# Five instead of four seven-product pairs in the up chunks of a split-precision decoder layer, the gate product moved to GpSimd

## The reference, cut to what matters

```python
D_MODEL, SEQ, D_FF = 2048, 256, 5632
def swiglu(x, wg, wu, wd):
    return (jax.nn.silu(x @ wg) * (x @ wu)) @ wd
...
f = swiglu(rmsnorm(h, ffn1_pre_g[l]), ffn1_wg[l], ffn1_wu[l], ffn1_wd[l])
h = h + FFN_RES_WEIGHT * rmsnorm(f, ffn1_post_g[l])
...  # a mixing part: sparse attention beside a convolution module, gated, times w_out
f = swiglu(rmsnorm(h, ffn2_pre_g[l]), ffn2_wg[l], ffn2_wu[l], ffn2_wd[l])
h = h + FFN_RES_WEIGHT * rmsnorm(f, ffn2_post_g[l])
```

## Time and profile before

| | us |
|---|---|
| median of 3 runs | 2064.92 (2064.72 to 2065.35) |
| the profiled execution, own time | 2066.93 |
| its span | 2065.3 |
| PE busy | 2051.3 (99%) |
| DVE busy | 1761.8 (85%) |
| ACT busy | 1163.3 (56%) |
| POOL busy | 97.2 (5%) |

### The profile page before, as it was taken

One profiled execution on the slowest core, in us unless ns is written; L12 is line 12 of the kernel. 1 busy time (PEld: TensorE's weight loads), 2 busy tenths in 40 slices (PEclk: granted clock), 3 DMA queues, 4 the chain that ended last, 5 costly groups with the idle time before them and its releaser, 6 DMA issues.

```text
span 2065.3 us, 26384 instructions
## 1 busy us (share of the span) xinstructions
PE 2051.3 (99%) x9238; PEld 1694.5 (82%) x9238; DVE 1761.8 (85%) x2039; ACT 1163.3 (56%) x1292; POOL 97.2 (5%) x134
## 2 busy tenths in 40 slices
PE   9999999999999999999999999999999999999998
PEld 7888888888888788888788888888888888888886
DVE  6999899989888858998687566878999899989897
ACT  6565665556555554444466444565656566666463
POOL 0010001000000000100000000000000000000000
PEclk9999999999999999999999999999999999999999
DMA  9777777765666666776555666567777777846664
GB/s 332 228 233 228 225 215 237 235 203 177 196 198 204 187 186 192 203 207 184 172 170 180 184 191 213 185 229 227 227 230 240 216 225 226 237 141 205 199 207 163
DMA packets 223516, 430.49 MB, mean 208 GB/s; under 512 B 16393, under 2 KB 16657, under 8 KB 223040
## 3 DMA queue, kind: packets, MB, share of 16 engines
q1 hardware_dynamic: 209904, 401.26, 60.6%
q0 software_dynamic: 13376, 27.98, 7.5%
q10 hardware_dynamic: 144, 0.04, 0.0%
HBM read 427.12 MB, written 2.11 MB: 208 GB/s over the span
## 4 chain that ended last, share of the span: by engine, by line
PE 93%; DVE 4%; DMA 1%; issue 1%; ACT 0%; SPq 0%; POOL 0%; DVEq 0%; ACTq 0%; POOLq 0%
PE banks L1772 91%; PE banks L1822 2%; DVE wlo L1079 2%; DMA raw<-in_ffn_wd_dram 1%; DMA raw<-in_ffn_wg_dram 0%; DVE res L1134 0%; DVE wsum L1270 0%; DVE h_lo L1390 0%; DVE wsum L1285 0%; DVE raw L1283 0%; DVE act_lo L1147 0%; DVE down_wsum_lo L1306 0%; ACT act_hi L599 0%; DVE nat L1262 0%; DVE comb L1323 0%
## 5 line engine op out<-in xcount | busy, mean ns | idle before, releaser
L584 ACT ACTIVATE whi<-raw 128x1024 fp32r<-128x1024 f32 x579 | 597.8, 1051 | 435.3 <-PE banks L1772 337.5
L1079 DVE TENSOR_TENSOR wlo<-raw,whi 128x1024 fp32r<-128x1024 f32 x580 | 690.3, 1216 | 152.5 <-ACT whi L584 150.1
L1772 PE MATMUL banks<-whi,act_hi 128*128 128x512 f32 x1568 | 507.8, 395 | 1.3 <-DVE wlo L1079 0.7
L1772 PE MATMUL banks<-whi,act_lo 128*128 128x512 f32 x1568 | 498.3, 389 | 0.0
L1772 PE MATMUL banks<-wlo,act_hi 128*128 128x512 f32 x1568 | 485.2, 389 | 0.0
L1772 PEld LDWEIGHTS banks<-whi,act_lo 128*128 128x128 f32 x1568 | 294.3, 188 | 62.2
L1772 PEld LDWEIGHTS banks<-wlo,act_hi 128*128 128x128 f32 x1568 | 294.2, 188 | 61.6 <-DVE wlo L1079 0.5
L1772 PEld LDWEIGHTS banks<-whi,act_hi 128*128 128x128 f32 x1568 | 291.1, 188 | 63.1 <-issue 4.7
L584 ACT ACTIVATE whi<-raw_deep 128x1024 fp32r<-128x1024 f32 x176 | 183.5, 1056 | 73.7 <-PE banks L1772 71.1
L1079 DVE TENSOR_TENSOR wlo<-raw_deep,whi 128x1024 fp32r<-128x1024 f32 x176 | 207.7, 1219 | 7.1 <-ACT whi L584 6.9
L716 ACT ACTIVATE wsum_hi<-wsum 128x1536 fp32r<-128x1536 f32 x80 | 119.0, 1488 | 149.6 <-PE banks L1772 88.0
(11 more groups left out here) (305 smaller groups left out, 2354.8 us busy)
## 6 DMA issues: line engine op xcount, KB each, us to landing
raw<-in_ffn_wd_dram SPq DMA_DIRECT2D x176, 512.0 KB, 4.8
raw<-in_w_in_dram SPq DMA_DIRECT2D x160, 512.0 KB, 3.7
raw<-in_ffn_wg_dram SPq DMA_DIRECT2D x88, 512.0 KB, 4.3
raw_deep<-in_ffn_wg_dram SPq DMA_DIRECT2D x88, 512.0 KB, 4.0
raw<-in_ffn_wu_dram SPq DMA_DIRECT2D x88, 512.0 KB, 5.4
raw_deep<-in_ffn_wu_dram SPq DMA_DIRECT2D x88, 512.0 KB, 5.4
raw<-in_w_out_dram SPq DMA_DIRECT2D x32, 512.0 KB, 4.3
raw<-in_ffn_wu_dram POOLq DMA_DIRECT2D x40, 256.0 KB, 5.6
```

The lines of the kernel that those rows point to most:

```text
L584: nc.scalar.activation(whi[:, j % RING, 0:kts * width], src[:, 0:kts * width], ACT.Copy).then_inc(hi_ready, 1)
L1079: nc.vector.tensor_tensor(wlo[:, j % RING, 0:n], raw_slot(j, deep)[0][:, 0:n], whi[:, j % RING, 0:n], ALU.subtract).then_inc(lo_ready, 1)
L1772: return nc.tensor.matmul(o, a, b, **kw)
```

## The change

1. `SEVEN` becomes (1, 2, 4, 5, 6): five seven-product pairs in each of the 20 summed chunks.
2. `wsum_hi` and `wsum_lo` get a second buffer each; ACT may write `wsum_hi` while PE still reads the one before. The second `wsum_hi` and raw slot 7 lie over `gpost`, so the load of `gpost` for the second block moves behind `pair_sums(1)`, POOL waits for the end of the up half before it loads `gpost`, and SP waits for the end of the mixing part's last tiles before it loads slab 7 of the second block.
3. The low parts of both slabs of a pair are one DVE operation of 2048 columns (`lo_pair`) for q = 0, 1, 2, 4, 5, 6; for q = 3 and 7 they stay apart, since slots 6 and 7 are no longer neighbours.
4. The gate product of a chunk runs on POOL, as one operation of 1024 columns with both operands in SBUF, behind the five DMAs of that chunk. The row factor is applied by ACT, with two more operations behind silu. For the last chunk of a block the product stays on DVE, as one operation.
5. ACT's copy of the transposed tile moves from pair 0 to pair 1.

```diff
-SEVEN = (1, 3, 5, 6)
+SEVEN = (1, 2, 4, 5, 6)
...
+        up_wsum_hi = [wsum_hi, sb("wsum_hi2", [P, 3, CW], f32r, over=o_gpost)[0]]
...
-        afull, _ = sb("afull", [P, TT, 2, P])
-        wsum_lo, _ = sb("wsum_lo", [P, 3, CW], f32r)
-        raw_deep, _ = sb("raw_deep", [P, DEEP - RING, SK * CW])
+        afull, _ = sb("afull", [P, TT, 2, P], over=o_bgate)
+        up_wsum_lo = [sb(f"wsum_lo{i}", [P, 3, CW], f32r)[0] for i in range(2)]
+        raw_deep, _ = sb("raw_deep", [P, 2, SK * CW])
+        raw_last = [sb("raw6", [P, SK * CW])[0], sb("raw7", [P, SK * CW], over=o_gpost + 4 * 3 * CW)[0]]
...
+        def up_buffer(group, i):
+
+            return (i + 1 - group) % 2
...
+                        if f and j == DEEP - 1:
+                            for buf in range(2):
+                                sp.wait_ge(acc_free[buf], MIX_FREED[buf])
                         load(j, w[:, k:k + SK, bass.ts(it, CW)], done, deep=True)
...
             def pair_sums(f):
 
+                def hidden(c):
+
+                    pool.wait_ge(silu_ready, SUMMED * f + c)
+                    pool.wait_ge(h_psum, UP_CHUNKS * f + c)
+                    nc.gpsimd.tensor_tensor(nat[:], comb[:, C12:C12 + TT, :], comb[:, C11:C11 + TT, :], ALU.mult).then_inc(hidden_ready, 1)
+
                 def one(c, group):
+                    first = isinstance(c, int) and c == 1
                     for q in SEVEN:
...
+                    if not first:
+                        hidden(c - 1)
 
                 summed_chunks(pool.Fori, one)
+                pool.wait_ge(mm_done, ffn_base[f] + UP_CHUNKS * UP_SLABS)
...
-            for buf in range(2):
-                pool.wait_ge(acc_free[buf], MIX_FREED[buf])
-            load_gpost(f2_post)
             root(7, rstd)
             pair_sums(1)
+            load_gpost(f2_post)
...
                     act.wait_ge(combined, combined_count(f, c, 5))
                     for t in range(TT):
-                        ins = nc.scalar.activation(comb[:, C11 + t, :], comb[:, C11 + t, :], ACT.Silu, scale=stat[:, RSTD + t:RSTD + t + 1])
+                        nc.scalar.activation(comb[:, C11 + t, :], comb[:, C11 + t, :], ACT.Silu, scale=stat[:, RSTD + t:RSTD + t + 1])
+                    for t in range(TT):
+                        ins = nc.scalar.activation(comb[:, C12 + t, :], comb[:, C12 + t, :], ACT.Copy, scale=stat[:, RSTD + t:RSTD + t + 1])
                     ins.then_inc(silu_ready, 1)
...
+                def weight_sums_hi(c, group, i):
+
+                    seven, opens = seven_before(f, c, i), isinstance(c, int) and c == 1 and i < 2
                     act.wait_ge(wsum_ready, 4 * seven + 4)
                     if not opens:
+                        act.wait_ge(wsum_used, seven - 1)
+                    elif f and i == 0:
                         act.wait_ge(wsum_used, seven)
-                    nc.scalar.activation(wsum_hi[:], wsum[:], ACT.Copy).then_inc(wsumhi_ready, 1)
+                    nc.scalar.activation(up_wsum_hi[up_buffer(group, i)][:], wsum[:], ACT.Copy).then_inc(wsumhi_ready, 1)
...
+            def lo_pair(j, ready):
+
+                dve.wait_ge(hi_ready, ready)
+                s = j % RING
+                src = raw[:, s:s + 2, :] if j % DEEP < RING else raw_deep[:, s:s + 2, :]
+                nc.vector.tensor_tensor(wlo[:, s:s + 2, :], src, whi[:, s:s + 2, :], ALU.subtract).then_inc(lo_ready, 2)
...
-                    for t in range(TT):
-                        ins = nc.vector.scalar_tensor_tensor(out=nat[:, t, :], in0=comb[:, C12 + t, :], scalar=stat[:, RSTD + t:RSTD + t + 1],
-                                                             in1=comb[:, C11 + t, :], op0=ALU.mult, op1=ALU.mult)
-                    ins.then_inc(hidden_ready, 1)
+                    nc.vector.tensor_tensor(nat[:], comb[:, C12:C12 + TT, :], comb[:, C11:C11 + TT, :], ALU.mult).then_inc(hidden_ready, 1)
...
-                        for j in 2 * q, 2 * q + 1:
-                            lo(j, n0 + j + 1, deep=True)
-                        if q == 6 and not first:
-                            hidden(c - 1)
+                        if q % RING < RING - 1:
+                            lo_pair(2 * q, n0 + 2 * q + 2)
+                        else:
+                            for j in 2 * q, 2 * q + 1:
+                                lo(j, n0 + j + 1, deep=True)
```

More of the change, by code:

```diff
@@ L184, in build @@
         asum, _ = sb("asum", [P, len(SEVEN), 4, P], over=o_asum_lo)
-        afull, _ = sb("afull", [P, TT, 2, P])
-        wsum_lo, _ = sb("wsum_lo", [P, 3, CW], f32r)
-        raw_deep, _ = sb("raw_deep", [P, DEEP - RING, SK * CW])
+        afull, _ = sb("afull", [P, TT, 2, P], over=o_bgate)
+        up_wsum_lo = [sb(f"wsum_lo{i}", [P, 3, CW], f32r)[0] for i in range(2)]
+        raw_deep, _ = sb("raw_deep", [P, 2, SK * CW])
+        raw_last = [sb("raw6", [P, SK * CW])[0], sb("raw7", [P, SK * CW], over=o_gpost + 4 * 3 * CW)[0]]
+        assert all(q % RING != RING - 1 for q in SEVEN)
         assert at[0] <= o_hlo, at[0]
@@ L726, in summed @@
                         hi_at(2 * q)
+                        if q == 1 and not first:
+                            hidden_copy(c - 2, group)
                         if q in SEVEN:
@@ L730, in summed @@
                         if q in SEVEN:
-                            weight_sums_hi(seven, first and f == 0 and q == SEVEN[0])
-                        if q == 0 and not first:
-                            hidden_copy(c - 2, group)
+                            weight_sums_hi(c, group, SEVEN.index(q))
                         if q == 4 and not first:
@@ L1302, in up_weight_sums, with weight_sums_lo @@
                     sums_of_lower_rows(2 * q, True).then_inc(wsum_ready, 2)
-                def weight_sums_lo(seven, low=wsum_lo):
+                def weight_sums_lo(seven, low, high=wsum_hi):
                     dve.wait_ge(wsumhi_ready, seven + 1)
-                    nc.vector.tensor_tensor(low[:], wsum[:], wsum_hi[:], ALU.subtract).then_inc(wsumlo_ready, 1)
+                    nc.vector.tensor_tensor(low[:], wsum[:], high[:], ALU.subtract).then_inc(wsumlo_ready, 1)
                 def combine(c, group):
@@ L1335, in summed @@
                             combine_last(c - 1, 1 - group, n0)
-                        for j in 2 * q, 2 * q + 1:
-                            lo(j, n0 + j + 1, deep=True)
-                        if q == 6 and not first:
-                            hidden(c - 1)
+                        if q % RING < RING - 1:
[3 more added lines that the diff above has]
+                                lo(j, n0 + j + 1, deep=True)
                         if q in SEVEN:
-                            weight_sums_lo(seven)
+                            buf = up_buffer(group, SEVEN.index(q))
+                            weight_sums_lo(seven, up_wsum_lo[buf], up_wsum_hi[buf])
                     combine(c, group)
@@ L1857, in start_phase, with seven_products @@
                         act_half(p, j + 2)
-            def seven_products(seven, ready, g, group, opens, closes, acts, sums, low):
+            def seven_products(seven, ready, g, group, opens, closes, acts, sums, low, high_sums=wsum_hi):
                 u, b = g + 1, 1 - group
@@ L1865, in seven_products @@
                                        for s, k in ((g, 0), (g, 1), (u, 0), (u, 1)))
-                bp, br, bz = ([t[:, n, :] for t in (wsum_hi, low)] for n in (P_SUM, R_SUM, Z_SUM))
+                bp, br, bz = ([t[:, n, :] for t in (high_sums, low)] for n in (P_SUM, R_SUM, Z_SUM))
                 m1, m5, m6, m7 = (banks[:, 4 * b + n, :] for n in (M1, M5, M6, M7))
@@ L1927, in summed @@
                             seven_products(seven_before(f, c, i), n0 + 2 * q + 1, 2 * q % RING, group, i == 0,
-                                           i == len(SEVEN) - 1, acts, [asum_hi[:, i], asum_lo[:, i]], wsum_lo)
+                                           i == len(SEVEN) - 1, acts, [asum_hi[:, i], asum_lo[:, i]], up_wsum_lo[up_buffer(group, i)],
+                                           up_wsum_hi[up_buffer(group, i)])
                         else:
```

3 lines of the change are left out of this document (2 added, 1 removed).

## The result

The changed kernel takes 2132.75 us (median of 4 runs, 2131.61 to 2133.70) against 2065.07 for the kernel before (median of 4): 1.0328 times as long, 95% interval 1.0310 to 1.0345. It is slower, as forecast, but by 67.7 instead of 47: the time lies 2.8 above the top of the range. The profiled execution took 2133.70 with a span of 2132.0, at a mean granted clock of 0.998.

A forecast was written before the change was run, and what follows sets the result against it. PE bounds the kernel before, DVE after. In 18 chunks 42.47 + 1.6 - 41.69 = 2.38, that is 42.8; with 2 and 2, +46.8, a median of 2112 us, range 2080 to 2130.

The forecast's parts named there:

- Parts 1 and 2: Summed chunk: the fifth pair cuts PE to 41.01 but brings DVE's work to 41.15, so DVE becomes the bound.
- Part 3: Summed chunk: DVE idles 1.3 before `combine`, so a chunk takes 42.47 and moving the product is worth nothing.
- the walk: DVE's operations followed from one `combine` to the next, through PE and ACT behind pair 6's low part: 42.47 a chunk.
- the sum: All terms added over the kernel: +46.8 on the profiled execution, giving a forecast median of 2112.
- Part 4: POOL's gate product holds DVE's two-operand operations up for 1.6 a chunk, scaled from POOL's selects.
- The first rival: POOL's product holds DVE longer, 2.0 to 3 a chunk; 2124 at 2.3, 2137 at 3; chance 0.24.
- Part 2's price of an R behind a low part: DVE's R directly behind a low part of sums: 1.84, 0.17 more, three times a chunk instead of once, +0.34.
- Part 5: The rest: buffers, ACT's extra work, added DMAs and the SP wait covered; first chunks 2 and down halves 2.
- First chunks: First summed chunks: a fifth set of activation sums, about +1 each, 2 in all.
- Down halves: Start of each down half: two ACT operations before the hidden tile's high part, +1.2 less 0.2, 2 for both.

The follow-up runs named there:

- pairs_only: Only the fifth pair and second buffers: changed kernel with low parts one slab at a time, product on DVE in its old two-operation form, no ACT row factor; 2094.55 us.
- pool_tiny: Changed kernel with POOL's gate product cut to 2 of 1024 columns, all waits and order kept; 2096.27 us.
- dve_product: Changed kernel with the gate product back on DVE as one operation behind pair 6's low part, row factor still on ACT; 2095.64 us.
- apart_pool: Changed kernel with the low parts of all pairs made one slab at a time, product still on POOL; 2118.18 us.
- pool_one_operand: Changed kernel with POOL's product replaced by two one-operand operations of 512 and 510 columns and a two-column product; 2109.08 us.
- waits_last: Changed kernel with DVE's wait for its own low part of sums moved behind the transfer waits ahead of R, and one wait dropped; 2129.20 us.
- four_pairs: Changed kernel with four seven-product pairs (1, 2, 4, 5), low parts one slab at a time, product still on POOL; 2068.29 us.
- probe_combine: Changed kernel with one more two-operand POOL product of 1024 columns beside `combine_last` in 18 chunks; 2137.79 us.
- alternating: Changed kernel with five pairs in odd chunks, four in even ones, low parts apart, product on DVE in old form, moved wait; 2067.81 us.
- pool_twice: Changed kernel with POOL's product made twice, the second waiting for the first; 2179.24 us.

## Why the prediction was right and wrong

**Parts 1 and 2, DVE becomes the bound: right.** DVE is busier than PE in the chunk, joined low parts take 2.28, and PE waits for DVE. The fifth pair alone already loses (pairs_only, 42.94 a chunk).

**Part 3, the walk of 42.47: right in mechanism, 0.31 short.** pool_tiny gives 42.78 in block 1, with the idle time before `combine` at 1.43 against 1.3. Of the 0.31, 0.19 lies behind the low part of pair 6 (5.36, not 5.17); the rest was not traced to one place. Over 18 chunks the term is +5.6. That moving the product is worth nothing was right for this kernel: dve_product and pool_tiny differ by 0.6. The joined low parts, which the sum counted as a gain of 0.42, are what makes it so, and they made the whole 14.6 slower (apart_pool): they hand PE its low part later. The walk contains that delay, but the prediction never priced it against the gain.

**Part 4, the blocking of 1.6: the step that failed most.** I scaled 0.78 ns a column from POOL's selects, which have one operand, to two operands. For one operand the figure holds (pool_one_operand: 0.38 to 0.40 for 512 columns in most chunks); for two of 1024 columns it is 1.0 to 1.1 ns a column read, and the hold measures 2.03 a chunk: +7.7 in all. The first rival, longer blocking, was therefore the case that came, at the lower edge of its 2.0 to 3. By the figure in the Trainium skill, "GPSIMD Engine Reference", section 3.1, the estimate was 2.2 for the product; the traces have 2.00 to 2.25 of hold, so it was nearer than the scaled select. The Trainium skill, "SBUF — State Buffer", section "SBUF: two separate sides", says that the side that starts first has the shared pair of ports for the whole instruction. That fits R beside the product that starts with it (2.25 of 2.40) but not the profiled lengths of the one-operand operations (0.38 of 1.48).

**Part 2's price of an R behind a low part, 1.84: short in block 2.** It is 1.95 to 2.06 there. Nothing in the sum told the two blocks apart, though the trace of the kernel before does, from start to start 2.05. Its timeline of DVE in block 2:

```profile
1597.61 1.75 DVE L1306 TENSOR_TENSOR wsum_lo<-wsum,wsum_hi 128x1536 fp32r<-128x1536 f32 x1
1599.66 0.69 DVE L1300 TENSOR_TENSOR wsum<-raw_deep 128x512 f32<-128x512 f32 x1 [0.30 <-DVE wsum_lo L1306]
```

The chunks of block 2 are 0.36 to 0.40 longer in the change and in pool_tiny: +3.6 over nine. waits_last shows that the waits in front of R are the cause, by their order or their number. R now meets such a wait three times a chunk, before once, so a cost of one or two tenths that did not matter before came onto the path.

**Part 5, the rest: mixed.** In the chunks no wait of DVE for the added DMAs or of PE for ACT shows, as forecast. First chunks: 4.2 against 2. With low parts apart they cost 0.80 and 1.50 (pairs_only) or 0.99 and 1.51 (apart_pool), and with four pairs nothing (four_pairs: -0.1 and 0), so about 2.4 belong to the fifth pair and its activation sums and most of the rest to the joined low parts. Down halves: 3.55 less 0.73, against 2. The 1.05 that ACT's two copies cost in each was near the forecast's 1.0; the rest is a lower clock in block 1. Timeline of PE in the changed kernel there, and below it the view by stage:

```profile
511.41 0.70 PE L1803 MATMUL banks<-whi,h_hi 128*128 128x512 f32 x2 [1.47 <-ACT whi L604]
...
514.43 1.05 PE L1803 MATMUL banks<-whi,h_lo 128*128 128x512 f32 x2
```

```profile
512.77:516.13 3.36, 3.36 (x8) 2.60 (x9) 3.36 (x4) 3.23 (x4) 0.00 (x0) 0.54 0.61 177
```

PE waits 1.47 for ACT, behind the two copies, where before it was 0.25. From 513.05 on, 1.6 after that wait, the granted clock is 0.50 for 3.4 (0.54 in this view, which begins a little earlier), its lower level of 1.2 GHz, and that costs 1.4. It does not always follow: the same wait of 1.47 or 1.48 stands in both blocks of nine traces, and in 14 of these 18 places the clock stays at 1.00 and the stretch takes 25.0 to 25.1; in four (the change, waits_last and four_pairs in block 1, apart_pool in block 2) it falls and the stretch takes 26.5. So this 1.4 is in part chance, and no run shows what decides it.

**The sum.** 46.8 + 7.7 + 5.6 + 3.6 + 2.2 + 1.6 - 0.7 = 66.8, against 66.7 measured in the span. All but the last of the misses have the same sign, and the range allowed for one of them, the blocking, at a time: its upper end of 2130 was worked out with every other term at its first value. The blocking alone, at 2.03 instead of 1.6, would have given 2064.9 + 18 x 2.81 + 4 = 2119.5, inside the range; it took the walk, the waits of block 2 and the first chunks as well to leave it.

## What to carry to other kernels

Before work is moved off a busy engine, find out whether its place lies on the path: here, with the low parts joined, 1.3 of product became 1.4 of idle time, and the same walk shows that joining two operations helps only where nobody waits for the first. A product on POOL beside a DVE that is the bound cost 2.03 of its 2.4 a chunk where DVE reads two SBUF operands; put such work beside operations that read PSUM (probe_combine: 0.3 a chunk), or where DVE has room (four_pairs: nothing). PE and DVE here are so close that a shift of work gives little: alternating balanced them, and won 0.05 a chunk.

## What the runs showed of the hardware that was not expected

- A POOL operation of 512 columns that reads one SBUF operand held a DVE operation with two for 0.38 to 0.41, in some chunks for 0.22; a product with two operands of 1024 columns for 2.00, and 2.25 where both start together. A DVE operation with one operand in PSUM was not held at all (2.28), nor did it hold the product (2.42).
- R started 2.04 behind the low part of the sums in block 2 when the wait met last stood ahead of three others, and 1.88 when it stood behind them and one of them was dropped.
- PE's waits of 0.93 leave the clock at 1.00 in the whole chunk. After one of 1.47 or 1.48 PE ran at the lower clock for 3.4 in four places out of 18, which cost 1.4 on top; with waits of 3.0 to 3.2 (pool_twice) it did in nine chunks out of 18, for 3.4 or 6.8.
